# Two projection slabs in half depth and double width, and four of sixteen expert rows added by VectorE from the first row on, in a two-layer hybrid decoder

## What is computed

```python
for layer in range(DEPTH):                        # 2
    h = rmsnorm(x, norm_mix[layer])
    x = x + (even_mixer(h, ...) if layer % 2 == 0 else odd_mixer(h, ...))
    x = x + peer(rmsnorm(x, norm_ffn[layer]), ...)
return rmsnorm(x, final_norm)
```

```python
qh = (xb @ w_q).reshape(128, 8, 2, 128)           # 8 heads, two halves
s = einsum('thpd,hpnd->thpn', qh, sub_keys)       # 128 keys a half
... top 16 of each half, top 16 of their 256 sums -> experts, gate
act = gelu(einsum('td,thkd->thk', xb, u_tab[experts]))
out = einsum('thk,thkd->td', gate * act, v_tab[experts])
```

## Time and profile before

| | |
|---|---|
| median of 3 runs | 3108.66 us (3108.12 to 3112.69) |
| the profiled execution | 3107.79 us |
| its span, first to last instruction | 3105.8 us |
| mean granted clock of PE | 0.963 of full speed |
| PE matmul busy | 2739.7 us (88%) |
| VectorE busy | 2206.6 us (71%) |
| ScalarE busy | 1524.3 us (49%) |
| POOL busy | 1293.6 us (42%) |
| moved by DMA | 1194.56 MB, mean 385 GB/s |

### The profile page before, as it was taken

How to read it: one execution, slowest core, us unless ns; L and a number is a source line. 1 busy time by engine, 2 the same in 40 slices (tenths; PEclk the granted TensorE clock), 3 DMA queues, 4 the chain that set the end, 5 groups by cost and what they waited for, 6 DMA issues and landing times.

```text
span 3105.8 us, 30287 instructions
## 1 busy us (share of the span) xinstructions
PE 2739.7 (88%) x8400; PEld 1460.4 (47%) x8400; DVE 2206.6 (71%) x5536; ACT 1524.3 (49%) x4088; POOL 1293.6 (42%) x1254
## 2 busy tenths in 40 slices
PE   8969899899898988989899899889999878787877
PEld 6446555344464555555465455555455422222222
DVE  0336557898757888888766788888876777677664
ACT  1434244786444565566444465556544444444443
POOL 0014234464444544445433455454453444444442
PEclk9989899999899999999999999999999999999999
DMA  8029899999999999999999999999999999999997
GB/s 283 14 98 401 350 398 400 410 364 379 424 421 425 421 396 391 377 394 412 409 424 426 424 416 376 390 386 394 411 423 424 427 427 427 427 423 425 425 425 316
DMA packets 194697, 1194.56 MB, mean 385 GB/s; under 512 B 21345, under 2 KB 32609, under 8 KB 56801
## 3 DMA queue, kind: packets, MB, share of 16 engines
q0 software_dynamic: 147456, 1073.81, 84.1%
q1 hardware_dynamic: 47072, 118.82, 10.0%
HBM read 1189.38 MB, written 2.10 MB: 384 GB/s over the span
## 4 chain that ended last, share of the span: by engine, by line
PE 46%; DMA 23%; DVE 17%; ACT 8%; issue 4%; POOL 2%; DVEq 0%; POOLq 0%; SPq 0%; ACTq 0%
PE ps L1821 25%; DMA region_g<-in_uv_dram,experts 21%; DVE region_g L1313 8%; PE ps L1651 5%; PE ps L1683 2%; PE ps L1712 2%; PE ps L1680 2%; DMA region_a<-in_w_even_dram 1%; PE ps L1730 1%; ACT x_res L947 1%; ACT L940 1%; DVE x_res L1322 1%; POOL region_g L674 1%; PE ps L1396 1%; PE ps L1519 1%
## 5 line engine op out<-in xcount | busy, mean ns | idle before, releaser
L1821 PE MATMUL ps<-region_g,x_res 128*128 128x512 f32 x3744 | 1824.2, 619 | 255.0 <-ACT x_res L947 239.9
L674 POOL DMA_INDIRECT region_g<-in_uv_dram,experts x1024 | 1155.9, 1129 | 1593.2 <-PE ps L1821 1310.7
L1313 DVE CUSTOM_DVE_ANT_0 region_g<-region_g,region_h 128x1024 f32<-128x1024 f32 x1024 | 1260.1, 1233 | 526.7 <-DMA region_g<-in_uv_dram,experts 516.4
L1821 PEld LDWEIGHTS ps<-region_g,x_res 128*128 128x128 f32 x3744 | 691.9, 195 | 1093.6 <-issue 576.2
L940 ACT ACTIVATE region_a<-region_a 128x1 f32<-128x1 f32 x1024 | 206.3, 202 | 1220.7 <-DVE region_a L1313 1213.7
L947 ACT ACTIVATE x_res<-ident,region_a 128x128 f32<-128x128 f32 x936 | 375.8, 402 | 30.6
L941 ACT ACTIVATE region_a<-region_a,gate 128x1 f32<-128x1 f32 x1024 | 301.6, 295 | 33.4
L1651 PE MATMUL ps<-region_a 128*128 128x256 f32 x1024 | 243.3, 382 | 1.2 <-issue 1.2
L1651 PEld LDWEIGHTS ps<-region_a 128*128 128x128 f32 x1024 | 196.2, 192 | 73.7 <-issue 52.0
L940 ACT ACT_TABLE_LOAD x128 | 164.2, 1283 | 13.8 <-DVE region_a L1313 11.6
L1680 PE MATMUL ps<-region_a 128*128 128x256 f32 x512 | 134.0, 392 | 1.0 <-DVE region_a L1149 1.0
(11 more groups left out here) (237 smaller groups left out, 2278.5 us busy)
## 6 DMA issues: line engine op xcount, KB each, us to landing
region_a<-in_w_q_dram SPq DMA_DIRECT2D x32, 1024.0 KB, 20.9
region_a<-in_w_odd_dram SPq DMA_DIRECT2D x32, 1024.0 KB
region_g<-in_uv_dram,experts POOLq DMA_INDIRECT x1024
region_g<-in_w_even_dram SPq DMA_DIRECT2D x8, 1024.0 KB, 10.3
region_a<-in_w_even_dram SPq DMA_DIRECT2D x8, 1024.0 KB, 15.7
region_a<-in_w_out_o_dram SPq DMA_DIRECT2D x8, 1024.0 KB
region_a<-in_keys_dram SPq DMA_DIRECT2D x32, 128.0 KB, 24.5
region_g<-in_w_out_e_dram SPq DMA_DIRECT2D x4, 1024.0 KB, 4.9
```

Of the source, the lines that this page charges most:

```text
L674: g.indirect_dma_start(out=gath[:, s % NBUF, :], out_offset=None, in_=uv[s // (2 * PHASE)], in_offset=bass.IndirectOffsetOnAxis(ap=experts ...
L1313: v.tensor_tensor_reduce(out=u_, in0=u_, in1=XNr[n // P_HEADS % 3], scale=1.0, scalar=0.0, op0=ALU.mult, op1=ALU.add, accum_out=dots[:, c: ...
L1821: i = t.matmul(PS[:, j, :], diag[:, pe_n(s) % NBUF, :], gath[:, s % NBUF, D_MODEL + j * 512:D_MODEL + (j + 1) * 512], start=first, stop=last)
```

## The change

Two things change.

The slabs F0 and F1 of the first mixer, for both pairs of blocks, take the form of F2 and F3: F0 is the first four chunks by 512 columns (kc, vc, ks, kw), F1 the last four, so a packet is 2 KB instead of 1 KB. PE now begins the sums of four banks with F0 (6 and 7 for ks and kw, 2 and 3 for kc and vc) and ends them with F1. A new event `k_half` says that F0 is used and its place free. ks and kw are complete after the second part of F1 (tick 22 instead of 18), and ScalarE's copy of them moves from tick 20 to 24. Since the keys now lie in banks 6 and 7, every part of the queries waits for the copy of the bank that it writes.

`ATTENDED` becomes all rows from 0 to 191, so rows 5, 7, 9 and 13 of each 16 in rows 0 to 95 (24 rows) take the VectorE way too.

```diff
@@ -37,7 +37,7 @@
 HEADS_AT, HEAD_PACE = 20, 19
 EVEN_AT = (-1000, 0)
 DVE_ROWS = ((), (5, 13), (5, 13), ())
-ATTENDED = range(96, 192)
+ATTENDED = range(192)
 ATTENDED_ROWS = (5, 7, 9, 13)
 FINAL_SLOTS = (3 * PHASE + 20, 3 * PHASE + 24, 3 * PHASE + BLOCK + 8)
 
@@ -240,7 +240,7 @@
         first_in = [sem(f"first_in{i}") for i in range(7)]
         lb_raw, lb_sig, masks_built = event("lb_raw"), event("lb_sig"), event("masks_built")
         n_ss, n_rs, n_xn, n_xT, n_hT = (event(n) for n in ("n_ss", "n_rs", "n_xn", "n_xT", "n_hT"))
-        f_half, f_done, f_out, g_done, g_out = (event(n) for n in ("f_half", "f_done", "f_out", "g_done", "g_out"))
+        k_half, f_half, f_done, f_out, g_done, g_out = (event(n) for n in ("k_half", "f_half", "f_done", "f_out", "g_done", "g_out"))
         pos_set, hid_zero, c_half, hid_done, hid_out, cmp_done, cmp_out = (
             event(n) for n in ("pos_set", "hid_zero", "c_half", "hid_done", "hid_out", "cmp_done", "cmp_out"))
         cs_done, cz_ready, ce_ready, pc_ready = (event(n) for n in ("cs_done", "cz_ready", "ce_ready", "pc_ready"))
@@ -372,7 +372,8 @@
 
         def even_slabs(q):
 
-            out_ = [(("F", q, i), ((f_done, 4 * q), (f_done, 4 * q + 1), (f_half, q), (f_done, 4 * q + 3))[i]) for i in range(4)]
+            out_ = [(("F", q, i), ((k_half, q), (f_done, 4 * q + 1), (f_half, q), (f_done, 4 * q + 3))[i])
+                    for i in range(4)]
             out_ += [(("G", q), (g_done, q))]
             out_ += [(("C", q, kv), ((c_half, q), (hid_done, q))[kv]) for kv in range(2)]
             out_ += [(("V", q, i), ((v_half, q), (v_done, 2 * q + 1))[i]) for i in range(2)]
@@ -447,8 +448,7 @@
                 if kind == "F":
                     if i >= 2:
                         return w_even[:, 4 * (i - 2):4 * (i - 2) + 4, TM_ALL:TM_ALL + 2 * HALF]
-                    lo = TM_ALL + (768, 512)[i]
-                    return w_even[:, :, lo:lo + HALF]
+                    return w_even[:, 4 * i:4 * i + 4, TM_ALL + 2 * HALF:TM_ALL + 4 * HALF]
                 if kind == "G":
                     return w_even[:, :, TM_UV:TM_ALL]
                 if kind == "C":
@@ -711,12 +711,12 @@
                     act.wait_ge(n_rs.sem, n_rs.at(2 * q + t))
                     a.activation(spare, X[:, 2 * q + t, :], ACT.Copy, scale=est[:, t, 2:3]).then_inc(n_xn.sem, 1)
                 for i in range(4):
-                    yield t0 + (20, 28, 40, 44)[i]
+                    yield t0 + (24, 28, 40, 44)[i]
                     act.wait_ge(f_done.sem, f_done.at(4 * q + i))
                     if i == 0:
-                        last = a.activation(kT[:, :, q * HALF:(q + 1) * HALF], v3(PS[:, 2, :], 2), ACT.Copy)
+                        last = a.activation(kT[:, :, q * HALF:(q + 1) * HALF], PS[:, 6:8, 0:HALF], ACT.Copy)
                     elif i == 1:
-                        src = v3(PS[:, 3, :], 2)
+                        src = PS[:, 2:4, 0:HALF]
                         if q == 0:
                             a.activation(kvl[:], src[:, :, HALF - CMP_STRIDE:HALF], ACT.Copy)
                         last = a.activation(kvc, src, ACT.Copy)
@@ -1384,26 +1384,28 @@
                     if q:
                         pe.wait_ge(n_hT.sem, n_hT.at(2 * q + r - 1))
                     row_transposes(XNr[2 - r * (q == 0)], n_xT, 4 if r and not q else 6)
-                for i in range(2):
-                    W = slab_of("F", q, i)[:, 0:KC * HALF].rearrange("p (c n) -> p c n", n=HALF)
+                for half_ in range(2):
+                    W = slab_of("F", q, half_)[:, 0:KC * HALF].rearrange("p (c n) -> p c n", n=2 * HALF)
                     for part in range(4):
-                        yield t0 + 12 + 8 * i + 2 * part
+                        yield t0 + 12 + 8 * half_ + 2 * part
                         if part == 0:
-                            slab_there(pe, "F", q, i)
+                            slab_there(pe, "F", q, half_)
                             pe.wait_ge(n_hT.sem, n_hT.at(2 * q + 1))
-                        o = part // 2
-                        for c in range(4 * (part % 2), 4 * (part % 2) + 4):
-                            k_ = t.matmul(PS[:, 2 + i, o * HALF:(o + 1) * HALF], W[:, c, o * P:(o + 1) * P], hTe[:, c, :],
+                        cols = (part + 2) % 4 * P
+                        for c in range(4 * half_, 4 * half_ + 4):
+                            k_ = t.matmul(PS[:, (6, 7, 2, 3)[part], 0:HALF], W[:, c % 4, cols:cols + P], hTe[:, c, :],
                                           start=c == 0, stop=c == KC - 1)
-                    k_.then_inc(f_done.sem, 1)
+                        if half_ and part % 2:
+                            k_.then_inc(f_done.sem, 1)
+                    if half_ == 0:
+                        k_.then_inc(k_half.sem, 1)
                 for half_ in range(2):
                     W = slab_of("F", q, 2 + half_)[:, 0:KC * HALF].rearrange("p (c n) -> p c n", n=2 * HALF)
                     for part in range(4):
                         yield t0 + 28 + 8 * half_ + 2 * part
                         if part == 0:
                             slab_there(pe, "F", q, 2 + half_)
-                        if part >= 2:
-                            pe.wait_ge(f_out.sem, f_out.at(4 * q + part - 2))
+                        pe.wait_ge(f_out.sem, f_out.at(4 * q + part // 2))
                         for c in range(4 * half_, 4 * half_ + 4):
                             k_ = t.matmul(PS[:, (6, 7, 2, 3)[part], 0:HALF], W[:, c % 4, part * P:(part + 1) * P], hTe[:, c, :],
                                           start=c == 0, stop=c == KC - 1)
```

## The result

The changed kernel took 3092.72 us, the median of 8 runs (3087.42 to 3101.13), against 3108.78 us for the kernel before (8 runs, 3105.77 to 3112.69). The ratio is 0.9946, 95% interval 0.9936 to 0.9956: some 17 us faster. The profiled execution took 3090.45 us, its span is 3088.5, so it lies 17.3 under the profiled one of before. Faster was the forecast, and the time is inside the range; but the forecast said 8.3 us, and it was twice that. The range holds the time only because it reached into the second rival (15 to 25 us, given a chance of 0.10); the band of the forecast itself, 7 to 14 us, was missed.

What follows compares the result with a forecast made beforehand. It took PE and DMA as both full from 227 to 552 us. Terms 3.5 + 1.8 + 4.8 - 1.8 = 8.3 us took the profiled 3107.8 to 3099.5 us; range 3089 to 3108.

Steps and rivals of the forecast that it cites:

- the second rival: Before row 96, nearly all of PE's saved time comes back: 15 to 25 us gained, 3083 to 3093; chance 0.10.
- Part A: Wider slabs F0 and F1 in the first mixer: no gain and cost 0, with cost ends 0 and 0.6 us.
- Term 1: Up to slab G: tick 18 comes 4.8 us earlier and G lands earlier; 3.5 us gained, ends 0 and 4.8.
- Term 2: After G: the DMA still stands, but gathers behind row 45 come earlier; 1.8 us gained, ends 0 and 6.9.
- Term 3: Stretch 484 to 516 us: eight rows leave PE and all the DMA loss returns; 4.8 us gained, ends 0 and 4.8.
- the sign row: Sign for the stretch that was 484 to 516 us: the DMA moves over 415 GB/s there.
- Term 4: Frictions: PE's waits for more slabs cost clock, and adds queue on VectorE; 1.8 us charged, ends 0 and 6.
- The first rival: G and the routing slabs land as before, only 484 to 516 gains: 0 to 5 us, 3103 to 3108; chance 0.33.
- The slower rival: Each of 24 VectorE adds delays a gather's issue on POOL by 1.28 us: slower, 3128 us; chance 0.07.
- The other signs: Changed profile: packet, add and product counts, G issued 4 to 5 us earlier, row 96 some 8 us earlier, tail unchanged.
- the 25.1 us of DMA loss: What the DMA lost against 427 GB/s in four stretches between 227 and 516 us, taken as all it could give.

Runs made afterwards that it cites:

- slabs_only: The changed kernel with rows 0 to 95 back on PE, so only the wider F0 and F1 slabs remain: 3108.5 us, ratio 1.0002 to the kernel before.
- rows_2_of_16: The changed kernel with only rows 5 and 13 of each 16 on VectorE in rows 0 to 95 (12 rows): 3104.3 us, ratio 0.9987.
- rows_from_48: The changed kernel with VectorE's rows only from row 48 on (12 of the 24): 3105.1 us, ratio 0.9985.
- rows_6_of_16: The changed kernel with rows 3, 5, 7, 9, 11, 13 of each 16 on VectorE in 0 to 95 (36 rows): 3097.3 us, ratio 0.9964.
- g_first_after: The changed kernel with slab G issued ahead of the eight small copies: 3093.0 us, ratio 0.9945 to the kernel before.
- c1_first: The changed kernel with G issued ahead of the copies and slab C1 loaded ahead of two routing slabs: 3093.2 us, ratio 0.9959.
- rows_only: The kernel before with the 24 rows moved to VectorE, slabs F0 and F1 as before: 3092.9 us, ratio 0.9948.
- rows_to_47: The changed kernel with VectorE's rows only in 0 to 47 (12 rows) and from 96 on: 3098.4 us, ratio 0.9968.

## Why the prediction was right, and where it was too small

- **Part A, cost 0:** right. slabs_only stands at 1.0002, and with both edits the time is that of the rows alone. What ended PE's first wait was VectorE's copy, before and after.
- **Term 1, tick 18 comes 4.8 us earlier:** right. The load behind it was issued at 280.58 instead of 287.56, 7.0 us earlier, of which 1.6 were there at row 0. 227 to 287 went from 402 to 426 GB/s, so the 3.5 us of DMA loss came back. The next step was wrong: I moved G's landing by what the DMA had lost ahead of it, to 371 to 373, and PE had G at 359.3. That step counted the DMA's bytes, not the turn of its packets. The rows that decide it: the 12 us without a gather, and the 945 packets ahead of G that passed in 5.5 us, where 1044 had taken 21.5.
- **Term 2, after G, 1.8 us of the 15.7:** this is the term that was mis-sized. I argued that PE would come to G still earlier and wait over 14.2 us, and that the eight buffers would then be full whatever else happened. The routing slab's wait in tick 33, which I had under frictions, comes first and turns this round: it keeps the gathers back while the packets ahead of G pass. PE did come to G earlier (355.7 for 361.6), but G came earlier by more. 372 to 404 gained 13.3 us (396 for 218 GB/s), and G's wait was 3.6 us. In the other kernels the wait for G stays near 14 us where PE waited little or not in tick 33 (rows_2_of_16, rows_from_48), and in rows_6_of_16, where G landed late.
- **Term 3, 484 to 516, 4.8 us:** the sign row is right (426 GB/s, over 415 was asked). Alone, these rows and the four from 53 to 61 gave 2.7 us up to row 96.
- **Term 4, frictions:** the places were named rightly, tick 33 and tick 60. PE stands 6.2 and 6.7 us there, and the granted clock is 0.84 in 300 to 332. What they cost is not measured: g_first_after and c1_first took single ones away and gained nothing, but the wait in tick 33 stayed in both, and c1_first got one of 8.3 us in place of that for C1.
- **The first rival,** that the DMA queue keeps it, is out: 416 for 386 GB/s. **The second,** that nearly all comes back, is what happened, 15 to 25 us by its own price, by the very way I had excluded: "the 15.7 us after G would have to go". I gave it 0.10 because eight buffers spoke against it; they are an argument only while PE waits at G and nowhere ahead of it. So the time lies in the range by the rival, and not by the mechanism that was forecast.
- **The slower rival,** an add holding the gather's issue, is borne out in kind and not in price. The changed kernel, lines L674 (230 to 530 us) and L1322, durations ns min/median/max:

```profile
L674 POOL DMA_INDIRECT region_g<-in_uv_dram,experts x101: 932/1001/1985, 233.0 to 526.6; - x101
...
L1322 DVE SCALAR_TENSOR_TENSOR x_res<-region_g,region_a,x_res x112: 1273/1280/1462, 244.2 to 2435.8; 128x1024 f32<-128x1024 f32 x112
```

  POOL waited 24.6 us for adds. Issues did get longer beside an add: of these 101 issues, the 15 that overlapped one have a median of 1490 ns, the other 86 of 953. This agrees with the Trainium skill, "SBUF — State Buffer", section "Who interferes with whom", on a VectorE instruction with two inputs in SBUF beside a GpSimd instruction that reads SBUF, if the issue is such a one. By the means, 1.40 and 1.17 us, it comes to 15 x 0.23 = 3.5 us, on an engine that stood 140.9 us waiting for PE (199.5 before, in a slightly longer stretch). The median of all issues, 1001 ns for 938, is no measure of it: rows_only, with the same 24 adds, has 947. With 36 rows the wait for adds grew to 74.3 us; whether it is a bound there is not shown.
- **The other signs:** 192,647 packets (192,649 forecast), 112 adds, 3648 products: right. Row 96 came 22 us earlier (8 forecast). G's issue moved 0.8 us, not 4 to 5, since the wait in tick 33 stands ahead of the matmuls that release it. From row 96 to the end nothing changed that the scatter lets one see; the four kernels that reached row 96 earliest took 2577.2 to 2581.6 us from there and the others 2571.5 to 2582.2, so a few us given back are not excluded.
- **A sum:** the 25.1 us of DMA loss are those of four stretches. 332 to 356 lost another 24 x (1 - 386/427) = 2.3, and 227 to 552 as a whole, by its own row, 325 x (1 - 389/427) = 28.9. It doesn't change the forecast, which added up the terms and not this.

**Open.** That the wait in tick 33 is what lets G through rests on the kernels side by side and on the packet counts; no kernel took that wait away and left all else. G's last packets come late: 90% of G had landed 124.4 us after row 0's dot product and the last at 133.1, the last of them mostly 0.35 us apart, as if a single DMA engine had them left. Why was not tried; it moves G's landing by several us from kernel to kernel, and with it the time. The 1.6 us before row 0 are no effect of the change: the first 64 projection matmuls took 14.05 us in the changed kernel and 15.68 before, but also 14.05 in rows_only, which has the slabs of before, and 16.00 in rows_to_47, which has the new ones.

## What to carry to other kernels

When two resources are near full, a stretch in which one of them stands idle is not a loss that can be struck out by itself: taken away at one wait it comes back at the next, as long as the other resource has all its work (two edits that removed the wait for G outright kept 3.5 us; the 24 rows off PE kept nearly five times that). When pricing when a late slab lands, count packets and who takes turns with them, not only bytes: what the other queue had outstanding at that moment moved G's landing by 15 us here. And an earlier short wait may be worth more than it costs, when it holds back the big transfers that the next slab would have to share the DMA with.

## What the runs showed that was not expected

- Where the gather queue and the slab queue both had work, they passed packet for packet (559 and 559 in 11 us, 1046 and 1044 in 21.5), however unlike their sizes: 4.06 MB against 0.52. A queue of 1120-byte packets beside one of 8 KB got an eighth of the bytes. With few gathers queued the slab queue passed 1094 packets in 8 us, 2.7 times as many per us.
- The rate fell while the small packets passed: 313 GB/s over those 8 us, with 545 of the 1343 packets under 512 bytes, against 427 in the best slices. Fewer gathers were queued then too, so the size of the packets may not be all of it.
- Gain was no smooth function of the rows moved: 8 rows 11.0 us up to row 96, 12 rows 7.3, 2.7 or 2.5 according to their place, 24 rows 20.3, 36 rows 13.6. By the ratios of the times, the gains are 12.7, then 9.9, 4.7 or 4.0, then 16.8 and 11.2; in these, 8 rows and 36 rows change places.
- G's landing, counted from row 0, differed by 6.4 us between two kernels that are the same up to there (133.1 and 139.5).
